# Finer first loads, fourteen conv taps on ScalarE, halved layer-norm sums and a last product by token tile

## The reference

```python
a = rms_norm(h, g_mix_pre[l])
proj = a @ w_in[l]                       # q, k, v (1024 columns each) and u (2048 columns)
attn = moba_attention(q, k, v)           # 8 heads of 128; one block of 256 keys: causal softmax with ALiBi
u = u + b_glu; val, gt = split(u)
h = val * sigmoid(gt)                    # 1024 channels
y = conv_general_dilated(h, w_dw, ...)   # 31 taps over time, one weight per tap and channel
y = silu(layer_norm(y + b_dw, ln_g, ln_b))
mixed = concatenate([attn, y]) @ w_out[l]
h = h + rms_norm(mixed, g_mix_post[l])
```

## Time and profile before

| | us |
|---|---|
| median of 3 runs | 1835.41 (1833.29 to 1836.21) |
| the profiled execution | 1836.25, its span 1834.6 |
| TensorE busy | 1805.0 of the span |
| VectorE busy | 1480.8 |
| ScalarE busy | 899.3 |

### The profile page before, as it was taken

The page is one execution under the profiler, slowest core; times in us unless marked ns, Lnnn a source line. Parts: engine busy times, 40 slices in busy tenths (PEclk is TensorE's granted clock), DMA queues, the critical chain, the costliest instruction groups (busy, mean ns, idle before and its releaser), DMA issues.

```text
span 1834.6 us, 26083 instructions
## 1 busy us (share of the span) xinstructions
PE 1805.0 (98%) x9856; PEld 1559.5 (85%) x9856; DVE 1480.8 (81%) x1718; ACT 899.3 (49%) x1165; POOL 112.9 (6%) x217
## 2 busy tenths in 40 slices
PE   8999999999999999999999999999999999999998
PEld 7889978788888888888888888888888888888986
DVE  6899988878888897889887877746788778897854
ACT  6444457555434443453344557523656545445453
POOL 0000000101000000000000000000111010000000
PEclk9999999999999999999999999999999999999999
DMA  8756546868787787778977865654656684878562
GB/s 305 247 165 195 161 138 250 311 201 313 244 290 248 264 272 232 227 258 304 247 252 263 314 231 176 225 187 138 223 194 225 252 295 152 272 246 276 194 225 97
DMA packets 191448, 426.92 MB, mean 233 GB/s; under 512 B 12656, under 2 KB 13040, under 8 KB 190320
## 3 DMA queue, kind: packets, MB, share of 16 engines
q1 hardware_dynamic: 158848, 323.73, 51.8%
q0 software_dynamic: 27648, 100.68, 16.7%
q10 hardware_dynamic: 4848, 1.07, 0.4%
HBM read 421.23 MB, written 4.21 MB: 232 GB/s over the span
## 4 chain that ended last, share of the span: by engine, by line
PE 82%; DVE 13%; ACT 2%; DMA 2%; issue 1%; SPq 0%; DVEq 0%; ACTq 0%; POOLq 0%
PE banks L2101 20%; PE banks L2148 13%; PE banks L2150 13%; PE banks L2149 13%; PE banks L2107 10%; DVE w_lo L1158 4%; DVE mod_sum L1369 4%; PE banks L2092 2%; PE banks L2094 2%; PE banks L2093 2%; PE banks L2474 2%; PE banks L2490 1%; PE banks L2211 1%; ACT w_hi L564 1%; PE banks L2465 1%
## 5 line engine op out<-in xcount | busy, mean ns | idle before, releaser
L564 ACT ACTIVATE w_hi<-raw 128x1024 fp32r<-128x1024 f32 x552 | 579.3, 1058 | 666.5 <-PE banks L2150 337.5
L1158 DVE TENSOR_TENSOR w_lo<-raw,w_hi 128x1024 fp32r<-128x1024 f32 x552 | 666.3, 1222 | 238.6 <-ACT w_hi L564 237.0
L2101 PE MATMUL banks<-a_pair,w_hi 128*128 128x512 f32 x1792 | 433.3, 393 | 9.4 <-DVE w_lo L1158 7.8
L2101 PEld LDWEIGHTS banks<-a_pair,w_hi 128*128 128x128 f32 x1792 | 329.3, 189 | 74.4 <-issue 7.4
L2148 PE MATMUL banks<-w_hi,b_hi 128*128 128x512 f32 x808 | 316.3, 391 | 0.4 <-DVE w_lo L1158 0.2
L1198 DVE SCALAR_TENSOR_TENSOR mod_sum<-mod_raw,silu_c,mod_sum 128x1024 f32<-128x1024 f32 x240 | 302.9, 1284 | 15.2 <-DMA mod_raw<-in_ev_mod_w 12.0
L2150 PE MATMUL banks<-w_hi,b_lo 128*128 128x512 f32 x808 | 314.5, 389 | 0.0
L2149 PE MATMUL banks<-w_lo,b_hi 128*128 128x512 f32 x808 | 314.4, 389 | 0.0
L2107 PEld LDWEIGHTS banks<-a_pair,w_lo 128*128 128x128 f32 x1792 | 230.8, 192 | 9.5 <-DVE w_lo L1158 0.6
L2107 PE MATMUL banks<-a_pair,w_lo 128*128 128x256 f32 x1792 | 234.7, 283 | 0.5 <-DVE w_lo L1158 0.5
L2148 PEld LDWEIGHTS banks<-w_hi,b_hi 128*128 128x128 f32 x808 | 151.7, 188 | 32.5 <-issue 0.6
(11 more groups left out here) (255 smaller groups left out, 1733.6 us busy)
## 6 DMA issues: line engine op xcount, KB each, us to landing
raw<-in_w_ff SPq DMA_DIRECT2D x128, 1024.0 KB, 6.6
mod_raw<-in_ev_mod_w POOLq DMA_DIRECT2D x96, 512.0 KB, 5.3
mod_raw<-in_od_mod_w POOLq DMA_DIRECT2D x96, 512.0 KB, 5.0
raw<-in_ev_w_in SPq DMA_DIRECT2D x40, 1024.0 KB, 5.6
raw<-in_w_in SPq DMA_DIRECT2D x39, 1024.0 KB, 5.1
raw<-in_od_w_in SPq DMA_DIRECT2D x32, 1024.0 KB, 6.0
raw<-in_w_out SPq DMA_DIRECT2D x16, 1024.0 KB, 5.4
raw<-in_ev_w_out SPq DMA_DIRECT2D x16, 1024.0 KB, 6.6
```

The source lines that it names most:

```text
L564: nc.scalar.activation(w_hi[:, s % SLOTS], raw[:, s // 2, KPS * (s % 2):KPS * (s % 2) + KPS, :], ACT.Copy).then_inc(hi_ready, 1)
L1158: nc.vector.tensor_tensor(w_lo[:, s % SLOTS], raw[:, s // 2, KPS * (s % 2):KPS * (s % 2) + KPS, :], w_hi[:, s % SLOTS].bitcast(F32), ALU.s ...
L2101: e = nc.tensor.matmul(out[:, f, :], w_hi[:, s % SLOTS, t, P * f:P * (f + 1)], rows[:, :, KPS * s + t, :], start=s == 0 and t == 0, stop=F ...
```

## The change

1. **First loads.** `x_cols` comes in six chunks (the chunk of tiles 4 to 7 becomes two), and all 8 steps of u0 have a load of their own (512 KB), where only steps 0 and 1 had.
2. **Scale row.** ACT and DVE split steps 0 and 1 of u1 before the root and the diagonals, steps 2 and 3 after; PE begins u1 and waits for `rstd_ready` only before the fourth bank of its first row.
3. **Query scale.** `queries_read` on ACT copies the queries unscaled in place of `columns_scaled` for qkv0 and qkv3. The scale of each query's token is in `token_s`, used as the scale of the exponential and for its bias; `dist_neg` is multiplied by the token's root once, before the first head.
4. **Conv.** Two groups ("quads") of four tiles. ACT multiplies taps 0 to 13 into two buffers, which are those of `mod_raw`, four instructions per tap; DVE adds each to the running sum of four tiles at once (`conv_sum`, 13 per quad) and does taps 14 to 30 as before (4 x 17 per quad).
5. **Modulation loads.** Halves 6 and on load when all 26 sums are done; 6, 7 and 8 are added one after the other behind the last `b_lo`.
6. **Layer norm sums.** DVE adds the tiles in halves (4, 2, 1) both for the mean and for the squares; PE needs one product in place of eight for `ln_var` and does n = 8 before it in place of after it. The sum for the mean is made in slot 4.
7. **End.** The last four steps of the last product go by token tile, and the residual is added tile by tile.

```diff
-X_CHUNKS = [(0, 2), (2, 4), (4, 8), (8, 12), (12, 16)]
+X_CHUNKS = [(0, 2), (2, 4), (4, 6), (6, 8), (8, 12), (12, 16)]
+ACT_TAPS = 14
+WIDES = ACT_TAPS - 1
+QUADS = CONV_TILES // 4
+def groups_at(point):
+    return min(point + (2 if point == 0 else 3 if point <= WIDES else 4), QUADS * ACT_TAPS)
...
+            for q in range(4):
+                for h in range(2):
+                    n = 2 * q + h
+                    if n < len(X_CHUNKS):
+                        load_columns(n)
+                    sp.wait_ge(split_done, n + 1)
+                    sp.dma_start(raw[:, q, KPS * h:KPS * (h + 1)], W[:, KPS * n:KPS * (n + 1), gate0]
+                                 ).then_inc(raw_in[q] if h else raw_half[q], 16)
...
-            load_mod("ev_gate", "ev", 2, 1, KT)
+            load_mod("ev_gate", "ev", 2, 1, 3)
+            pool.wait_ge(conv_wide, QUADS * WIDES)
+            load_mod("ev_gate", "ev", 2, 3, KT)
...
+            def tap_group():
+                n = product_now[0]
+                q, t = n // ACT_TAPS, n % ACT_TAPS
+                if t == 0:
+                    act.wait_ge(glu_ready, q + 1)
+                if n < 2:
+                    act.wait_ge(mod_acc, MOD_STEP0["ev_gate"] + 6)
+                else:
+                    act.wait_ge(conv_wide, WIDES * ((n - 2) // ACT_TAPS) + max((n - 2) % ACT_TAPS, 1))
+                for c in range(4):
+                    ct = 4 * q + c
+                    dst, src, w = tap_products[n % 2][:, c, :], conv_in[:, ct, t:t + T], col("w_dw", TAPS * ct + t)
...
+                        e = nc.scalar.activation(dst, src, ACT.Copy, scale=w)
+                e.then_inc(conv_product, 1)
...
+            split_hi(1, range(2))
             root("mix")
+            split_hi(1, [2])
             act.wait_ge(rstd_row, 1)
             nc.scalar.activation(ln_rstd[:], aux[:, 3, 0:T], ACT.Copy).then_inc(rstd_ready, 1)
+            split_hi(1, [3])
...
+            split_lo(1, (0, 1))
             dve.wait_ge(ident_in, 16)
             dve.wait_ge(tok_summed, 1)
             mean_eps("mix", aux[:, 2, 0:TT], norm_s[:, 6:8])
             token_diagonals()
+            split_lo(1, (2, 3))
...
+            def conv_ahead(b, point):
+                for m in range(4):
+                    ahead, s = b + (m >= 2), (2 * m + 4) % STEPS
+                    split_lo(ahead, [s])
+                    if 0 < point + m != WIDES:
+                        conv_sum()
+                    split_lo(ahead, [s + 1])
+                    if point + m in (0, WIDES):
+                        if point:
+                            conv_taps(quad_taps - tap_now[0])
+                        conv_sum()
+                    conv_taps(2 if point + m == WIDES else 5)
...
-            nc.vector.tensor_reduce(ln_rstd[:], conv_y.rearrange("p c t -> p t c"), AX.X, ALU.add).then_inc(conv_total, 1)
...
-            halves("ev_gate", 6, 2)
+            dve.wait_ge(conv_sq_ready, 1)
+            channels_added(conv_sq, square_total)
...
-            halves("ev_gate", 8, 1)
+            halves("ev_gate", 6, 3)
...
-            out_step(6)
-            out_step(7)
-            pe.wait_ge(conv_sq_ready, 1)
+            for n in range(6, 9):
+                out_step(n)
+            pe.wait_ge(square_total, 1)
             pe.wait_ge(head_copied, HEADS)
-            channel_sums(ln_var, conv_sq)
-            for n in range(8, 30):
+            nc.tensor.matmul(ln_var, ones[:], ln_rstd[:], start=True, stop=True).then_inc(ln_sum, 1)
+            for n in range(9, 30):
...
-            add_to_residual(range(3), [0])
+            add_to_residual(range(NBLK), [0])
             gained(2 * (3 * NBLK - 1), NBLK - 1, acc[1], None, [1])
             dve.wait_ge(acc_free, 2 + ACC["odo"] + 4)
             post_scale("odo", 1)
-            add_to_residual([0], [1])
-            add_to_residual([3], [0])
-            add_to_residual(range(1, NBLK), [1])
+            add_to_residual(range(NBLK), [1])
...
-                product(BLOCK["odo"] + n, ACC["odo"] + n, acc[n % 2], step_tokens, a_hi, a_lo, p_ready, FT, 0, by_tile=n == 3)
+                product(BLOCK["odo"] + n, ACC["odo"] + n, acc[n % 2], step_tokens, a_hi, a_lo, p_ready, FT, 0, by_tile=4 * (n == 3))
```

More of the change, by code:

```diff
@@ L267, in build_program @@
         cols_in = sem("cols_in")
-        raw_first = sem("raw_first")
+        raw_half = [sem(f"raw_half{q}") for q in range(4)]
         head_cols = [sem(f"head_cols{i}") for i in range(TT)]
@@ L2152, in step_tokens, with last_steps @@
                 return last
-            def last_steps(steps, a2, hi, lo):
+            def last_steps(steps, a2, hi, lo, splits=None):
                 for tt in range(TT):
                     for s, slot in steps:
+                        if splits is not None and tt == 0:
+                            pe.wait_ge(split_done, splits + s)
                         for t in range(KPS):
@@ L2354, in head_slot1 @@
                     qkv_step(3 + (6 * m + k) // STEPS, (6 * m + k) % STEPS)
-            def channel_sums(sums, rows):
-                for k in range(CONV_TILES):
-                    e = nc.tensor.matmul(sums, ones[:], rows[:, k, :], start=k == 0, stop=k == CONV_TILES - 1)
-                e.then_inc(ln_sum, 1)
             for m in range(HEADS):
```

176 lines of the change are left out of this document (118 added, 58 removed).

## The result

The changed kernel takes 1845.40 us, the median of 5 runs (1842.49 to 1846.84), beside 1835.41 of the kernel before (1833.29 to 1838.45) on the same chip: 1.0050 times as long, with an interval from 1.0036 to 1.0065. Forecast were 1835.6 us and a range of 1828.5 to 1840.5. The profiled execution took 1845.61 us, its span is 1843.6. PE's busy time is the same 1805.0 us as before, so the 9.0 us by which the span is longer are idle time of PE.

The account below looks back on a forecast made before the run. PE was taken as the bound, busy 1805.0 of 1834.6 us. Terms netted +1.1 - 0.95 = +0.15 us on the profiled 1836.25, or 1835.6 on the median, with an 8-in-10 range of 1828.5 to 1840.5.

Parts of the forecast that it names:

- First loads: In u0: step 2 can start after 2.25 MB instead of 3.0 MB; gain between 0 and 2.7 us, taken as 1.5.
- Scale row: At u1: start 5.9 us ahead including 1.5 from earlier, 2.3 to 2.4 more from full clock; 8.3 ahead at u2.
- Conv in u2: From DVE's u2 splits to the sigmoids' sum: 24.5 us, 3.7 more; PE 4.6 ahead at u3's step 4, idle 5.3.
- PE stays the bound: In qkv0 to qkv2: per two steps DVE has 5.4 to 5.6 us of work, PE 5.8 (5.4 for qkv2).
- Head slots: At head slot 3: the 3.77 us wait and the low clock behind it go, 6.1 us in all; 8.6 ahead.
- Layer norm: From ln_mean to n = 12: the lead grows from 8.6 to 9.6 us, with PE waiting there.
- Three halves in a row: Before n = 16: half 8's load lands in 8.9 us, PE idles 8.4, low clock costs 2.3; 1.1 us behind.
- End: At the last product and residual: DVE is free when tile 1's squares are ready; gain 0.95 us.
- Short landing: Rival, before n = 16: half 8's load lands in 5.4 us; 3.35 us faster, 1832.1 us; chance 0.20.
- covered wait: Rival, at n = 16: landing in 4 to 5 us and 2.7 from first loads; about -7 us, 1828.5; chance 0.10.
- ACT and DVE wait for each other: Rival, in the conv: sums and products wait for each other, two buffers between; +6 us, 1841.6; chance 0.14.
- late keys: Rival, at head slot 3: DVE is still late for the keys, keeping up to 6.1 us; 1841.7 us; chance 0.07.

Follow-up runs that it names:

- e_spread: e_early with three conv taps on DVE per point of u2 to qkv2 instead of five, the others in head slots 3 to 6; 1827.0 us, ratio 0.9959.
- e_half6: The changed kernel with half 6 of ev_gate added before the layer norm's scale; 1839.9 us, ratio 1.0035.
- e_both: The changed kernel with the first loads of the kernel before and half 6 added before the layer norm's scale; 1836.49 us, ratio 1.0014.
- e_row: The kernel before with only the new order at the scale row, modulation halves 0 and 1 moving behind the splits; 1830.03 us, ratio 0.9978.
- e_rowend: e_row plus the last four steps of the last product by token tile and the residual tile by tile; 1828.59 us, ratio 0.9970.
- e_spread4: e_spread with four conv taps on DVE at each point instead of three; 1822.93 us, ratio 0.9934.
- e_early: The changed kernel with the old first loads and halves 6 and 7 both added before the layer norm's mean; 1831.06 us, ratio 0.9984.
- e_table: e_both with the distance table's products and the token scales moved from before head 0 into u1; 1837.02 us, ratio 1.0011.
- e_fine_x: e_spread with the columns in six chunks, those of tiles 8 to 11 behind the weights of steps 4 and 5; 1827.95 us, ratio 0.9962.

## Why the prediction was wrong

Step by step, as the prediction put them:

- *First loads* (bounds 0 and 2.7 us, taken 1.5): the step that failed first. It cost 2.7 us in the profile, 2.6 to 3.4 by the medians with and without, and 0.1 to 1.3 in the kernel of e_spread, where it can't be told from nothing. "Step 2 of u0 can start after 2.25 MB in place of 3.0 MB" is what was wrong: ACT's rounding of step 2 waits for the load of step 3 too, which comes after 3.0 MB as before. With this wait my own count gives nothing for steps 2 and 3 and a loss of 1.3 us for step 4, since step 5's load stands behind 0.5 MB more; so the bounds should have been a loss of 1.3 us and nothing, and not a gain. In the profile ACT rounded step 2 1.8 us and step 4 2.7 us later than before. What goes beyond the count is in part the hole in the rate and in part scatter (step 2 is rounded 1.4 us later in this profile than in e_half6's); how much is either stays open.
- *Scale row* (u1's start 4.4 us earlier without the first loads): right, and even 5.2 in e_both and e_row's profile. But "loses no clock: 2.3 to 2.4 us more" brought nearly nothing. From u1's start to the first sum of the gated channels it takes 28.2 us before (38.59 to 66.83) and 28.0 in e_both (33.40 to 61.38), in spite of full clock. PE has a new wait there of 1.16 us, for `w_lo` in step 4. From u1's start to the wide products at 55.45 us it takes 22.05 us, and to the same products before (61.36) it took 22.77: 0.7 less, where full clock should have made it 2.3 less, so 1.6 us went at that wait. DVE's wait of 0.38 us for the load of a modulation half takes most of the rest. The lead at u2 is 5.4 to 5.9 us where I had 6.8 without the loads. Alone this part is worth 4 to 6 us (e_row).
- *Conv in u2* (24.5 us, 3.7 more than before) and *in u3* (2.2 more): right. From DVE's first split of u2 to the sum it is 24.13 us (69.20 to 93.33). From that split to PE's step 4 of u3 it takes 30.6 us where it took 27.3, and from there to step 4 of qkv0 26.0 where it took 24.4: 3.3 and 1.6 us more. The forecast said that PE idles 5.3 us in u3; it is 4.39.
- *PE stays the bound* ("In qkv0 to qkv2 DVE has 5.4 to 5.6 us of work for two steps, PE 5.8") and "All else (the scaled table, 1 us of DVE before the first head) lies under PE": the second step that failed. The point is 5.39 us, as said. But DVE had no reserve when it came in: its split at 124.55 us was the one PE waited for. Before it had none either, and its split behind head 0 (190.81, 1.23 long) was done just as PE wanted it (192.09). From the one split to the other DVE now takes 72.5 us where it took 69.3: some 2.3 more in the twelve points, 1.14 of idle for a late rounding at the second quad's start and 0.7 for the table, less 1.14 for the one query scaling that is gone. PE's work there is the same, and it waited 3.05 us. I looked at the share per point and not at what was left at its end.
- *Head slots* (wait and low clock of slot 3 gone, 6.1 us): right. From 6.2 us behind at 198.31 PE is level with before behind slot 3, at the products with `ident` at 264.96 us (265.02 before).
- *Layer norm* (1.0 us of gain): right, 1.3 us (n = 12 starts at 303.59 for 304.87); the wait forecast before n = 12 for `b_lo` is 1.38 us, stands before n = 11 and is for a split.
- *Three halves in a row*: right in every number but the absolute time. Landing 9.0 for 8.9, idle PE 8.30 for 8.4, then products of 0.63 us. The feed-forward part starts another 3.5 us later than n = 16 did, 2.3 of it forecast, 0.9 a longer wait before 364.74. The rule of the Trainium skill named in the prediction (turns between the queue rows; page "DMA: Bandwidth & Descriptors", section "Queues, rings and completion order") would have had 5.4 us; the row says 9.0.
- *End* (0.95): 1.8 us by the profile (10.8 behind at the feed-forward part, 9.0 at the end), 1.4 by the medians of e_rowend and e_row. The last product with the gain starts 3.67 us before DVE's end in place of 4.31, and the rest is won before it.

The sum: 4.2 us of the first loads, 0.4 at u1's start and 1.9 that u1 does not regain make 6.5 at u2; the conv gives back 1.0; head 0 costs 3.05; the tail some 1.2 more, and the end gives back 0.9. That is 8.85 us, by which the span is longer than forecast (9.0 less 0.15).

Of the rivals, none was this. *ACT and DVE wait for each other* (1841.6) and the late keys (1841.7) came nearest in number, but by the wrong mechanism: the points took 5.39 us, and 4.59 with two taps less on DVE (e_spread), so ACT did not hold them; and slot 3 had no wait. *Short landing* and *covered wait* fell with the 9.0 us.

## What to carry to other kernels

When an engine that is full is given less work per step, look at the reserve with which it enters and leaves the stage; work moved within it (the table) gains nothing, and only work moved out to where it has time does (e_spread4, 8.1 us less than e_early by the medians). With two buffers that a slow load fills, each use moved behind a long stage delays one later load, so undo all of them (with the old first loads 6.3 us with one moved, e_both, and 11.7 with both, e_early). When a load is cut in two, follow every wait on its semaphore: here the consumer of the first part still waited for the second, and a byte count up to the first part was worth nothing. Keep the rows of the loads long, and give a loss its place in the range.

## What the runs showed of the hardware

- A second load of 512 KB on POOL's queue beside SP's 2 MB took 9.0 us, as the row of before had it at this place. It was the most reliable number of the forecast.
- The clock falls at different times behind the same wait. At slot 3 PE waited 3.75 us in e_row and the four score products took 1.65 us; in e_rowend it waited 3.76 and they took 0.92. The mean granted clock of the five microseconds from 235 us, in e_row and then in e_rowend (the columns are those of rows 1):

```profile
235.00:240.00 5.00, 5.00 (x14) 3.91 (x13) 4.96 (x12) 0.70 (x2) 0.00 (x0) 0.53 0.32 91
```

```profile
235.00:240.00 5.00, 5.00 (x17) 3.92 (x16) 5.00 (x12) 0.09 (x1) 0.00 (x0) 0.66 0.34 93
```

- The wait of 3.05 us behind head 0 had no low clock behind it in the changed kernel (1.00 from 200 to 205 us), and one in e_both with 3.02 us (0.66 from 195 to 200). Shorter waits do it too: behind 2.29 us in e_table the clock was 0.69 from 195 to 200 us, and behind the waits in u3 of 2.52 us in e_spread and 2.53 in e_fine_x the eight products took 2.11 and 3.26 us. So the length of a wait from 2.3 to 3 microseconds does not settle whether slow products follow it.
